# The projection's token chunks: 384, 384 and 320 columns instead of 364, 362 and 362, each from 88 bytes past a multiple of 256

## What is computed

```
xp = _layer_norm(x_prompt, ln_in_w, ln_in_b)          # and x_sample likewise
z  = x @ w_in + b_in                                  # 1024 -> 5528 columns, all of q, k, v, gates
mix: sparse attention (compressed, selected and window branches), mLSTM, forgetting attention
y  = einsum('blmd,blmd->bld', sigmoid(gates), branch_m @ w_branch[m])   # three branches, merged
x  = layer_norm(alpha * x + y @ w_out)
x  = layer_norm(alpha * x + moe(x))                   # top group, then top 2 of its 4 experts, 16 in all
```

## Time and profile before

| | |
|---|---|
| median of 3 runs | 1519.19 us (1518.12 to 1521.09) |
| profiled execution: span from first to last instruction | 1512.9 us |
| TensorE busy | 1378.2 us, 91% |
| VectorE, ScalarE, GpSimd busy | 613.6, 491.9, 301.9 us |
| projection (59 to 644 us): TensorE busy | 579.2 of 585.0 us |
| granted TensorE clock, mean over the span | 0.956 of 2.4 GHz |

### The profile page before, as it was taken

How to read it: one execution, slowest core, us unless ns; L and a number is a source line. 1 busy time by engine, 2 the same in 40 slices (tenths; PEclk the granted TensorE clock), 3 DMA queues, 4 the chain that set the end, 5 groups by cost and what they waited for, 6 DMA issues and landing times. The chain is left out here.

```text
span 1512.9 us, 23347 instructions
## 1 busy us (share of the span) xinstructions
PE 1378.2 (91%) x8773; PEld 1165.0 (77%) x8773; DVE 613.6 (41%) x1608; ACT 491.9 (33%) x920; POOL 301.9 (20%) x406
## 2 busy tenths in 40 slices
PE   5999999999999999978889879989985999999945
PEld 4999999999898889946665655668875888888812
DVE  6222212212323214044677547864563333333317
ACT  5422221222122321136455644320011434333233
POOL 5211150020102000003333200001043222323203
PEclk9999999999999999969999989989986999999977
DMA  7244393262625225780004037742126788888755
GB/s 210 71 155 146 124 243 116 59 182 70 185 64 158 70 64 73 191 228 15 1 2 161 23 102 257 238 155 74 63 75 180 254 281 269 279 275 255 264 203 201
DMA packets 188961, 228.28 MB, mean 151 GB/s; under 512 B 47607, under 2 KB 157303, under 8 KB 187487
## 3 DMA queue, kind: packets, MB, share of 16 engines
q1 hardware_dynamic: 176270, 186.25, 40.6%
q0 software_dynamic: 12592, 40.71, 8.5%
HBM read 167.89 MB, written 60.19 MB: 151 GB/s over the span
## 5 line engine op out<-in xcount | busy, mean ns | idle before, releaser
L1255 PE MATMUL psum<-proj_x_hi,proj_w_hi 128*128 128x362 f32 (+1 forms) x1056 | 356.8, 338 | 1.5 <-POOL proj_x_lo L1461 0.8
L1255 PE MATMUL psum<-proj_x_hi,proj_w_lo 128*128 128x362 f32 (+1 forms) x1056 | 346.3, 328 | 0.0
L1255 PE MATMUL psum<-proj_x_lo,proj_w_hi 128*128 128x362 f32 (+1 forms) x1056 | 346.3, 328 | 0.0
L1255 PEld LDWEIGHTS psum<-proj_x_hi,proj_w_hi 128*128 128x128 f32 x1056 | 199.2, 189 | 8.3 <-issue 2.2
L1255 PEld LDWEIGHTS psum<-proj_x_lo,proj_w_hi 128*128 128x128 f32 x1056 | 199.5, 189 | 0.0
L1255 PEld LDWEIGHTS psum<-proj_x_hi,proj_w_lo 128*128 128x128 f32 x1056 | 199.0, 188 | 0.0
L1380 DVE TENSOR_TENSOR proj_w_lo<-proj_w_raw,proj_w_hi 128x1024 fp32r<-128x1024 f32 x44 | 54.0, 1227 | 271.4 <-ACT proj_w_hi L1288 271.3
L1317 ACT ACTIVATE proj_sig<-psum,proj_bias 128x362 f32<-128x362 f32 (+1 forms) x72 | 40.2, 563 | 238.6 <-PE psum L1255 229.0
L2112 PE MATMUL psum<-branches_t,merge_branch_w 128*128 128x362 f32 (+1 forms) x288 | 91.2, 480 | 8.1 <-DMA merge_branch_w<-in_w_branch 8.1
L2617 PEld LDWEIGHTS psum<-moe_xgt,expert_gate_w 128*128 128x128 f32 x512 | 85.0, 193 | 13.2 <-issue 13.2
L2617 PE MATMUL psum<-moe_xgt,expert_gate_w 128*128 128x192 f32 x512 | 91.9, 334 | 0.7 <-ACT moe_xgt L2661 0.7
(11 more groups left out here) (465 smaller groups left out, 2184.6 us busy)
## 6 DMA issues: line engine op xcount, KB each, us to landing
proj_w_raw<-in_w_in SPq DMA_DIRECT2D x43, 512.0 KB, 5.0
expert_gate_w<-in_moe_w_gate SPq DMA_DIRECT2D x16, 1024.0 KB, 5.5
expert_up_w<-in_moe_w_up SPq DMA_DIRECT2D x16, 1024.0 KB, 11.0
expert_down_w<-in_moe_w_down SPq DMA_DIRECT2D x16, 1024.0 KB, 8.4
merge_sig<-gate_scratch SPq DMA_DIRECT2D x24, 544.0 KB, 3.9
gate_scratch<-proj_sig SPq DMA_DIRECT2D x48, 181.0 KB, 2.0
final_pair<-expert_rows SPq DMA_DIRECT2D x8, 1024.0 KB, 11.7
feature_scratch<-proj_feat SPq DMA_DIRECT2D x13, 512.0 KB, 3.0
```

Source lines behind the costliest of these rows:

```text
L1255: mm = nc.tensor.matmul(k.ps[u % RING][:, 0:w], b[wt][:, x % 2, kk, :], b[xx][:, kk, a0:a0 + w], start=(kk == 0 and i == 0), stop=(kk == K ...
```

## The change

`MCH` becomes (0, 384), (384, 384), (768, 320), the widths of the groups of the start. The row of a `kk` in `x_hi` and `x_lo` becomes XW = 1152 words (4608 bytes, 18 x 256), of which the tokens take 1088 from word X0 = 22 on. So token 0, 384 and 768 stand at bytes 88, 1624 and 3160 of a row, each 88 past a multiple of 256. `x_chunk` gives a chunk's place, in the matmuls as in `spread` and `low`. `sig` and the merge's `part` grow to 384 columns; the merge, the gate stores and the evacuations follow `MCH`. `width` is no longer needed.

```diff
--- before.py
+++ after.py
@@ -70,7 +70,8 @@
 V_SEL, V_WIN, V_FOX = 0, 64, (128, 192, 256, 320)
 V_MV, V_MO = 384, 644
 
-MCH = [(0, 364), (364, 362), (726, 362)]
+MCH = [(0, 384), (384, 384), (768, 320)]
+X0, XW = 22, 1152
 
 
 def rows(t):
@@ -1058,7 +1059,7 @@
     NX, RAW, XF, SIG, RING = 2, 3, 3, 3, 4
     st, b, s = phase(k, "proj", dict(
         lnw_col=[P, KD], lnb_col=[P, KD], stats=[P, 12], mean_var=[P, NT, 2], var_eps=[P, NT], rstd=[P, NT],
-        x_hi=[P, KD, T], x_lo=[P, KD, T], w_raw=[P, RAW, KD, P], w_hi=[P, 2, KD, P], w_lo=[P, 2, KD, P], bias=[P, NB], sig=[P, SIG, 364]),
+        x_hi=[P, KD, XW], x_lo=[P, KD, XW], w_raw=[P, RAW, KD, P], w_hi=[P, 2, KD, P], w_lo=[P, 2, KD, P], bias=[P, NB], sig=[P, SIG, 384]),
         ["const_loaded", "tables_loaded", "ln_cols_loaded", "ln_rows_loaded", "stats_done", "mv_done", "ve_done", "rstd_done", "xhat_done", "xt_psum", "x_full_done", "x_hi_done", "x_lo_done",
          "xscaled", "xnorm_done", "bias_loaded", "bias_scaled", "w_hi_done", "w_lo_done", "mm_done", "evac_done", "turned", "turn_copied", "new_copied", "dec_out"]
         + [f"x_loaded{i}" for i in range(NT)] + [f"xnorm_stored{i}" for i in range(NX)] + [f"w_loaded{i}" for i in range(RAW)]
@@ -1074,11 +1075,11 @@
     early_loads, side_sync, side_tensor, side_scalar, side_vector, side_gpsimd = side_programs(k, sb, ss, zd, zg, td, a, br_dec)
     ahead |= {n: right.enter_context(nc.sbuf_tensor(f"ahead_{n}", shape, F32, side="right")) for n, shape in dict(bias=[P, H, SEQ + P], nq=[P, 2, SEQ], ksel=[P, SEQ]).items()}
     groups = [(0, 3), (3, 3), (6, 3)]
-    width = lambda t0, cnt: sum(rows(t0 + j) for j in range(cnt))
     src = lambda t: io["x_prompt"][0, t * P:(t + 1) * P, :] if t < PT else io["x_sample"].rearrange("b t d -> (b t) d")
 
     units = [(0, 0), (1, 0), (0, 1), (1, 1), (0, 2), (1, 2)] + [(x, n) for x in range(2, NB) for n in range(3)]
     at = {x: u for u, x in enumerate(units)}
+    x_chunk = lambda part, n, kk: b[part][:, kk, X0 + MCH[n][0]:X0 + MCH[n][0] + MCH[n][1]]
     end = {x: at[(x, 2)] for x in range(NB)}
     name = lambda x: ZBLOCKS[x][0] if x < NZ else "gate"
     block_of = {zb: x for x, zb in enumerate(ZBLOCKS)}
@@ -1252,7 +1253,7 @@
                     if u < 6 and x == 0:
                         pe.wait_ge(s["x_lo_done"], n * KD + kk + 1)
                     for i, (wt, xx) in enumerate((("w_hi", "x_hi"), ("w_hi", "x_lo"), ("w_lo", "x_hi"))):
-                        mm = nc.tensor.matmul(k.ps[u % RING][:, 0:w], b[wt][:, x % 2, kk, :], b[xx][:, kk, a0:a0 + w], start=(kk == 0 and i == 0), stop=(kk == KD - 1 and i == 2))
+                        mm = nc.tensor.matmul(k.ps[u % RING][:, 0:w], b[wt][:, x % 2, kk, :], x_chunk(xx, n, kk), start=(kk == 0 and i == 0), stop=(kk == KD - 1 and i == 2))
                 mm.then_inc(s["mm_done"], 1)
 
             def turn(zb, g):
@@ -1291,15 +1292,14 @@
 
             def spread(g):
                 nonlocal nx
-                t0, cnt = groups[g]
-                w = width(t0, cnt)
+                w = MCH[g][1]
                 for kk in range(KD):
                     act.wait_ge(s["xt_psum"], nx + 1)
                     if nx >= XF:
                         act.wait_ge(s["x_lo_done"], nx - XF + 1)
                     ps = k.ps[4 + nx % 2][:, 0:w]
                     nc.scalar.activation(b["x_full"][:, nx % XF, 0:w], ps, ACT.Identity, bias=b["lnb_col"][:, kk:kk + 1], scale=b["lnw_col"][:, kk:kk + 1]).then_inc(s["x_full_done"], 1)
-                    nc.scalar.activation(b["x_hi"][:, kk, t0 * P:t0 * P + w], ps, ACT.Identity, bias=b["lnb_col"][:, kk:kk + 1], scale=b["lnw_col"][:, kk:kk + 1]).then_inc(s["x_hi_done"], 1)
+                    nc.scalar.activation(x_chunk("x_hi", g, kk), ps, ACT.Identity, bias=b["lnb_col"][:, kk:kk + 1], scale=b["lnw_col"][:, kk:kk + 1]).then_inc(s["x_hi_done"], 1)
                     nx += 1
 
             nsig = 0
@@ -1455,10 +1455,9 @@
                 nonlocal nx
                 for _ in range(n):
                     g, kk = divmod(nx, KD)
-                    t0, cnt = groups[g]
-                    w = width(t0, cnt)
+                    w = MCH[g][1]
                     pool.wait_ge(s["x_hi_done"], nx + 1)
-                    nc.gpsimd.tensor_tensor(b["x_lo"][:, kk, t0 * P:t0 * P + w], b["x_full"][:, nx % XF, 0:w], b["x_hi"][:, kk, t0 * P:t0 * P + w].bitcast(F32), ALU.subtract).then_inc(s["x_lo_done"], 1)
+                    nc.gpsimd.tensor_tensor(x_chunk("x_lo", g, kk), b["x_full"][:, nx % XF, 0:w], x_chunk("x_hi", g, kk).bitcast(F32), ALU.subtract).then_inc(s["x_lo_done"], 1)
                     nx += 1
 
             for t in range(NT):
@@ -2060,7 +2059,7 @@
 
     nc, io = k.nc, k.io
     UNITS, RING = 3 * KD, 4
-    st, b, s = phase(k, "merge", dict(sig=[P, RING, T], branch_w=[P, RING, 2, P], part=[P, 2, 364], whole=[P, 2, T]),
+    st, b, s = phase(k, "merge", dict(sig=[P, RING, T], branch_w=[P, RING, 2, P], part=[P, 2, 384], whole=[P, 2, T]),
                      ["proj_mm", "sig_done", "gated", "summed", "y_hi_done", "y_lo_done"] + [f"br_loaded{m}_{n}" for m in range(3) for n in range(3)] + [f"sig_loaded{i}" for i in range(RING)] + [f"bw_loaded{i}" for i in range(RING)])
     N = UNITS * 3
     added_upto = lambda u: sum(1 for x in range(u + 1) if (x // 3) % 3)
```

## The result

Medians of six runs each on one chip: 1518.84 us before (1517.81 to 1521.09; the three of the table above are among them), 1525.62 after (1524.14 to 1529.6). The ratio is 1.0041, 95% interval 1.0026 to 1.0057. So the changed kernel is slower by 5 to 7 us, where 3.5 us less was forecast, and its 1525.6 us lie above the range that ended at 1524.

What follows compares the result with a forecast made beforehand. TensorE was taken as the bound, the projection lasting as long as its back-to-back matmuls. Span 1512.9 - 2.9 (pitch) - 0.6 (start) = 1509.4 us, plus 6.3 gives 1515.7 us; range 1506 to 1524.

Steps and rivals of the forecast that it cites:

- the range that ended at 1524: Whole kernel: measured time expected between 1506 and 1524 us, with some 8% below and 8% above.
- That only the pitch could move the end, and that it goes in unshortened: Projection: only the distance between matmul starts moves its end, in full; 2.9 us off over 1008 triples.
- Evacuations, stores and the merge: Work beside the projection's matmuls and the later merge: put at 0, the merge with 0.3 us either way.
- The start, 0.6 us off: Units 0 to 5, 20 to 59 us: unit 2 0.2 us more, units 4 and 5 0.8 less, others hidden.
- I take 13.0 for all three, since the start is what the edit makes common: Projection matmuls: 13.0 ns beyond the columns' time for each chunk, 38.9 together against 41.8, 2.9 us off.
- The range, 9.2 to 15.6 a matmul: Projection: bounds on the surplus in ns, from 14.4 us off to 5.0 us on.
- 2% of the chances: Projection pace: something unforeseen, such as a step up of a whole 6.7 ns, slower; 2%.
- Rival C: Projection: chunks ending 88 past a multiple of 256 read broken pieces at both ends; surplus 15.6, 1523.6 us; 23%.
- Rival A: Projection: surplus does not follow the start and goes on averaging near 14; 1518.6 us; 20%.
- Rival B: Projection: with all chunks alike from 88, every unit settles at the 160.0 pace; 1504.2 us; 20%, part-way included.
- The median of the runs is 6.3 us above this span, which I keep: Whole kernel: 6.3 us between profile span and median kept, taking the 1509.4 us span to 1515.7 us.

Runs made afterwards that it cites:

- e2: Kernel before, its widths 364, 362, 362 kept, x moved so chunks start 88, 8 and 176 bytes past a multiple of 256: 1518.9 us, ratio 0.9989.
- e1: Changed kernel with X0 = 0, so the widths 384, 384, 320 begin on multiples of 256 bytes: 1519.2 us, ratio 0.9994 to before.
- e10: Changed kernel with X0 = 16, every chunk beginning 64 bytes past a multiple of 256: ratio 0.997 to before; run again, 1518.7 us, 0.9992.
- e13: Changed kernel with X0 = 6, every chunk beginning 24 bytes past a multiple of 256: ratio 1.0033 to before.
- e14: Changed kernel with X0 = 8, every chunk beginning 32 bytes past a multiple of 256: ratio 1.000 to before.
- e4: Kernel before, cut anew per block from the third on: chunk 0 300 to 382 columns, chunk 1 always 384, chunk 2 the rest; no total time given.
- e7: Kernel before, chunk 2 always 348 columns from byte 2960, chunk 0 swept from 330 to 412, chunk 1 between; no total time given.
- e9: Kernel before with chunks of 348, 392 and 348 columns in all blocks: 1522.25 us, ratio 1.0009.
- e3: Kernel before, cut anew per block from the third on: chunk 0 330 to 412 columns from byte 0, chunk 1 always 362, chunk 2 the rest: 1522.66 us.
- e5: Changed kernel with the split weights also moved, to 24 bytes past a multiple of 64, and x_lo shortened: 1536.39 us, one run.
- e8: Kernel before, rows of 1104 words, chunk 0 always 348 columns from byte 16, chunk 1 swept from 330 to 412, chunk 2 the rest: 1524.04 us.
- e6: Changed kernel with each product written from column 22 of its PSUM bank on: 1524.74 us, one run.

## Why the prediction was wrong, step by step

- **That only the pitch could move the end, and that it goes in unshortened**: right. 7.3 ns by 1008 triples, or the 6.8 us that the traces show, is of the size of the measured 5 to 7 us. Evacuations, stores and the merge were put at 0, and the account closes without them to within the interval. (The six merge matmuls of the earlier trace rows are two of 362 and four of 364 columns, 303 to 306 ns apart; the 0 stands, 91.9 us for 92.0.)
- **The start, 0.6 us off**: 0.56 in the first traces, but the sum was lucky. Units 4 and 5 gave 0.71 of 0.8, and unit 2 took 0.2 more, as forecast. Unit 3 was not hidden: it takes 8.66 us in both executions of the changed kernel, 8.40 and 8.39 in those of the kernel before. The rest is unit 0, 9.64 us for 10.07, and that is no effect of the edit, since the old widths take 9.11 in e2 and the new ones 10.07 in e1. Without it units 1 to 5 gave 0.2 us.
- **"I take 13.0 for all three, since the start is what the edit makes common"**: this step failed. The surpluses became 17.2, 16.6 and 15.3, 49.1 together for the 38.9 of the sum; 10.2 ns by 1008 is 10.3 us, the whole of the miss (1525.6 for 1515.7). I gave chunk 2's good pace to its start at 88; e2 put 364 columns there and they did not gain (166.9 against 166.5). What could have been seen: one start had been measured at one width only, so the row could not tell start from width, nor from end. The rows of 512 columns, 12.7 and 15.6, were a check of the width at unknown starts, and I called the agreeing one support.
- **The range, 9.2 to 15.6 a matmul**: too low at its upper end. The mean surplus of the changed kernel is 49.1/3 = 16.4, above every row from which I had made the bound. A pace that can step by 6.7 ns should have had one step of room on either side; it had 2% of the chances instead.
- **Rival C**, broken pieces at both ends: the nearest in direction and size (15.6 for 16.4, 1523.6 us for 1525.6). Its mechanism is not shown. In e2 the 364 columns begin 88 and end 8 bytes past a multiple of 256, broken at both ends, and lose 0.4 ns; only 384 and 320 columns lose (e1, e10, e13). The Trainium skill (SBUF — State Buffer, "Door 1: The DMA port swizzle") stood beside it with lines of 16 bytes: by it starts 0, 32 and 64 are alike and 24 and 88 are worse, and e1, e14, e10, e13 and the change itself came out in that order. But the measurements speak against 16 bytes as the granule: in e4 starts of 16 and 48, on such a line, go at 175.4 and 176.3 ns, no better than 8 and 56 with 175.5 and 176.2. And 364 columns from 88 in e2 don't follow it.
- **Rival A**, the address does not count: false for these widths, nearly true for 364 (166.5 and 166.9) and 362 (163.2 to 164.8). **Rival B**, all units settle at the 160.0 pace from 88: false. Its premise that one and the same chunk has several paces holds (e7, e9), and 384 columns from 88 have two as well: 37 of chunk 0's units settle at 177.8 ns and 5 at 173.3. That the way a unit is entered picks among them is likely, but not shown.
- **"The median of the runs is 6.3 us above this span, which I keep"**: that was a quick execution and no fixed share. Where one run has both numbers (e3 1522.66 us and a span of 1521.0, e5 1536.39 and 1534.7, e8 1524.04 and 1522.4), the time is 1.6 to 1.7 us above the span, and no more than that lies before the first and after the last instruction. The sum was not harmed, since both sides got the same 6.3, but the span of one execution can lie some 5 us off the others.

Open remains what picks among the stable paces of a chunk, why 362 and 364 columns hardly mind their start, whether it is the start or the end that costs, and the mechanism itself. That the reads of x and of the weights set the surplus fits e5, e6, e13 and the pace of exactly 362/1.2 at the low clock, but it is argued: no run measured a read.

## What to carry to other kernels

Where a stage is nothing but matmuls back to back, read the distance between starts, unit by unit, and multiply its change by the number of matmuls: here 7 ns made 7 us. For split float32 operands cut in chunks of 384 and 320 columns, let x start on a multiple of 64 bytes (7 us of 1519 here) and leave the weights there too; for other widths and types nothing is shown, and no gain over 364 and 362 is to be had by it. Before a row is used as the price of an address, ask what else is particular to it (width, end, the unit before), and before one good unit is made a plan, look whether the same shape keeps that pace in its other units.

## What the runs showed of the hardware that was not expected

- The paces of these f32 split matmuls settle at multiples of 6.67 ns (16 columns' worth) or at fractions between them: 160.0, 163.3, 166.7, 173.3, 177.8, 180.0. From byte 0 in e3 the surplus over columns/2.4 is 13.3 ns at 336, 352, 368, 384 and 400 columns. Elsewhere it need not be: 400 columns from byte 2752, also a multiple of 64, go at 183.3 in e4.
- 384 columns: 173.3 ns from byte 64, 176.7 from byte 24, 320 columns 146.7 and 149.2. With the weights moved as well (e5, one run): 156.0 for 320.
- Several paces are stable for one and the same chunk: 348 columns from byte 2960 at 153.3 or 160.0 ns, 392 from byte 1392 at 173.3 or 180.0.
- At the granted clock's lower level, 1.2 GHz, 362 columns take 301.7 ns, so no surplus. The Trainium skill (TensorE: Matmul & The Clock Gate, "Back-to-back issue gap") has the columns over 1.2 there, with which this agrees. At the upper level it has the columns over 2.4 plus 2.5 ns, for an isolated matmul; in a stream with a weight load before each, it says, both set the spacing. Every pace of this case is 8.3 ns or more above its columns there (348 columns at 153.3 are the nearest).
